# A decoder layer's mixture-of-experts output: rows accumulated in the output tensor instead of an internal copy of it

## The reference

```python
x = x + einsum('bse,ed->bsd', mix, w_out)            # "x2": one row for each token
h = rmsnorm(x, ln2_w)
logits = h @ w_router + b_router                      # 32 experts
top_vals, top_idx = top_k(logits, 4); gates = softmax(top_vals)
# for each expert e, over the tokens that chose it:
gu = h @ w_gate_up[e] + b_gate_up[e]
g = minimum(gu[:, :1024], 7); u = clip(gu[:, 1024:], -7, 7)
y = ((u + 1) * g * sigmoid(1.702 * g)) @ w_down[e] + b_down[e]
x[token] += gate * y                                  # four such rows are added to each token
```

## Time and profile before

| | us |
|---|---|
| median of three runs | 2045.23 (2040.22 to 2046.78) |
| the profiled execution | 2041.34 |
| its span, from first to last instruction | 2039.6 |
| TensorE matmul busy | 1899.4 (93%) |
| VectorE busy | 1277.3 (63%) |
| ScalarE busy | 1050.6 (52%) |
| GpSimd busy | 402.3 (20%) |
| DMA, mean | 246 GB/s, 501.81 MB |

### The profile page before, as it was taken

The page is one execution under the profiler, slowest core; times in us unless marked ns, Lnnn a source line. Parts: engine busy times, 40 slices in busy tenths (PEclk is TensorE's granted clock), DMA queues, the critical chain, the costliest instruction groups (busy, mean ns, idle before and its releaser), DMA issues.

```text
span 2039.6 us, 51127 instructions
## 1 busy us (share of the span) xinstructions
PE 1899.4 (93%) x20629; PEld 1761.9 (86%) x20629; DVE 1277.3 (63%) x2642; ACT 1050.6 (52%) x1442; POOL 402.3 (20%) x302
## 2 busy tenths in 40 slices
PE   6999988979968999999999999999999999989982
PEld 4777756658858999999999999999999999988982
DVE  4543647764378555566665567776677687776681
ACT  5574335552105444455555556555665665655661
POOL 4010000001002111111111112213243243333241
PEclk9999999989968999999999999999999999999996
DMA  4111010015377788889999899999999999999994
GB/s 141 52 42 42 21 62 1 2 46 189 137 260 246 262 280 280 272 274 304 306 306 306 303 310 312 312 327 336 371 354 372 371 353 371 370 351 369 369 346 114
DMA packets 251771, 501.81 MB, mean 246 GB/s; under 512 B 13025, under 2 KB 33809, under 8 KB 251585
## 3 DMA queue, kind: packets, MB, share of 16 engines
q1 hardware_dynamic: 231376, 446.73, 60.4%
q0 software_dynamic: 20256, 51.73, 11.7%
q10 hardware_dynamic: 48, 2.10, 0.3%
HBM read 471.16 MB, written 52.43 MB: 257 GB/s over the span
## 4 chain that ended last, share of the span: by engine, by line
PE 54%; DVE 4%; DMA 4%; issue 4%; SPq 2%; ACT 1%; POOL 0%; DVEq 0%; ACTq 0%; POOLq 0%
PE E_p_d L1945 22%; PE E_p_g L1934 5%; PE E_p_g L1937 5%; PE E_p_g L1936 5%; PE E_p_u L1937 5%; PE E_p_u L1934 5%; PE E_p_u L1936 5%; DMA E_w_st<-in_w_down 4%; DVE E_w_lo L1775 3%; SPq L1570 2%; PE E_p_t L1916 2%; PE E_p_t L1901 2%; ACT E_w_hi L1689 1%; DVE E_up L1835 0%; DVE E_gate L1823 0%
## 5 line engine op out<-in xcount | busy, mean ns | idle before, releaser
L1775 DVE SCALAR_TENSOR_TENSOR E_w_lo<-E_w_st,E_w_hi 128x2048 f16<-128x2048 f32 x260 | 594.8, 2288 | 60.3 <-ACT E_w_hi L1689 56.6
L1689 ACT ACTIVATE E_w_hi<-E_w_st 128x2048 f16<-128x2048 f32 x260 | 493.0, 1906 | 142.4 <-PE E_p_g L1937 95.7
L1945 PE MATMUL E_p_d<-E_a_f,E_w_st 128*128 128x160 f32 (+6 forms) x4096 | 536.3, 291 | 21.7 <-DMA E_w_st<-in_w_down 13.4
L1945 PEld LDWEIGHTS E_p_d<-E_a_f,E_w_st 128*128 128x128 f32 x4096 | 521.2, 193 | 29.2 <-DMA E_w_st<-in_w_down 16.2
L1934 PE MATMUL E_p_g<-E_x_hi,E_w_hi 128*128 128x160 f16 (+6 forms) x2048 | 373.0, 224 | 7.2 <-DVE E_w_lo L1775 7.2
L1934 PE MATMUL E_p_u<-E_x_hi,E_w_hi 128*128 128x160 f16 (+6 forms) x2048 | 371.7, 223 | 5.0 <-DVE E_w_lo L1775 5.0
L1936 PE MATMUL E_p_g<-E_x_lo,E_w_hi 128*128 128x160 f16 (+6 forms) x2048 | 373.0, 224 | 0.0
L1937 PE MATMUL E_p_g<-E_x_hi,E_w_lo 128*128 128x160 f16 (+6 forms) x2048 | 372.9, 224 | 0.0
L1937 PE MATMUL E_p_u<-E_x_hi,E_w_lo 128*128 128x160 f16 (+6 forms) x2048 | 371.6, 223 | 0.0
L1936 PE MATMUL E_p_u<-E_x_lo,E_w_hi 128*128 128x160 f16 (+6 forms) x2048 | 371.6, 223 | 0.0
L1633 POOL DMA_INDIRECT sum_rows<-E_y_rows,E_idx_out x66 | 169.0, 2561 | 596.6 <-ACT E_y_rows L1707 586.4
(11 more groups left out here) (375 smaller groups left out, 2758.7 us busy)
## 6 DMA issues: line engine op xcount, KB each, us to landing
E_w_st<-in_w_gate_up SPq DMA_DIRECT2D x130, 2048.0 KB, 15.7
E_w_st<-in_w_down SPq DMA_DIRECT2D x64, 2048.0 KB
A_w_st<-in_w_in SPq DMA_DIRECT2D x20, 512.0 KB, 3.9
sum_rows<-C_x SPq DMA_DIRECT2D x10, 512.0 KB, 5.8
A_x_rows<-in_x SPq DMA_DIRECT2D x8, 512.0 KB, 8.2
C_x_res<-in_x SPq DMA_DIRECT2D x8, 512.0 KB, 4.7
x_rows<-C_x SPq DMA_DIRECT2D x8, 512.0 KB, 5.0
h_rows<-C_h SPq DMA_DIRECT2D x8, 512.0 KB, 4.6
```

The lines of the kernel that those rows point to most:

```text
L1689: act.activation(w_hi[c % RI][:], staged(c % NG), ACT.Copy, scale=SW).then_inc(hi_s, 1)
L1775: dve.scalar_tensor_tensor(out=w_lo[c % RI][:], in0=staged(c % NG), scalar=SW, in1=w_hi[c % RI][:], op0=ALU.mult, op1=ALU.subtract, accum_ ...
L1945: ins = pe.matmul(banks[:, h, 0:w], staged(c)[:, k, h * P:(h + 1) * P], x[:, k, 0:w], start=h == 0 and k == 0, stop=k == KT - 1, skip_grou ...
```

## The change

The output projection's rows are written to the output tensor itself, and the experts' scatters accumulate there. `sum_rows` with its spare rows is gone. The scatter's bounds check gets the limit 1023 and leaves out lanes beyond it instead of calling them an error, so the padding lanes, which still point to rows 1024 and up, are written nowhere. Stage F is gone. The number of transfers, their waits and their order in stage E stay.

```diff
                     sp.dma_start(m.x2_d[q * P:(q + 1) * P, :], x2[q % 2][:]).then_inc(x2_out[q % 2], 16)
-                    sp.dma_start(m.sum_d[q * P:(q + 1) * P, :], x2[q % 2][:]).then_inc(sum_out[q % 2], 16)
-                    if q < NB:
-                        sp.dma_start(m.sum_d[S + q * P:S + (q + 1) * P, :], x2[q % 2][:]).then_inc(sum_out[q % 2], 16)
+                    sp.dma_start(a.out[0, q * P:(q + 1) * P, :], x2[q % 2][:]).then_inc(sum_out[q % 2], 16)
...
-                sp.wait_ge(sum_out[i], 16 * (T // 2 + 1))
+                sp.wait_ge(sum_out[i], 16 * (T // 2))
...
-                    dve.wait_ge(sum_out[t % 2], 16 * (t // 2 + 1))
+                    dve.wait_ge(sum_out[t % 2], 16 * (t // 2))
...
-            token_max, row_max = pool.to_reg(S - 1), pool.to_reg(S + CHUNK - 1)
+            token_max = pool.to_reg(S - 1)
...
-                    pool.indirect_dma_start(m.sum_d, bass.IndirectOffsetOnAxis(ap=idx_out[:, b:b + 1], axis=0),
-                                            y_rows[:, b, :], None, bounds_check=row_max, oob_is_err=True,
+                    pool.indirect_dma_start(a.out[0], bass.IndirectOffsetOnAxis(ap=idx_out[:, b:b + 1], axis=0),
+                                            y_rows[:, b, :], None, bounds_check=token_max, oob_is_err=False,
                                             compute_op=ALU.add).then_inc(scattered, 16)
...
-                    pool.dma_start(m.sum_d[0:S, :], m.x2_d).then_inc(restored, 16)
+                    pool.dma_start(a.out[0], m.x2_d).then_inc(restored, 16)
...
-def stage_f(nc, m, a):
...
-            sp.dma_start(a.out[0, 0:S // 2, :], m.sum_d[0:S // 2, :]).then_inc(done[0], 16)
...
-            act.dma_start(a.out[0, S // 2:S, :], m.sum_d[S // 2:S, :]).then_inc(done[1], 16)
...
-    m.sum_d = nc.dram_tensor("sum_rows", (S + CHUNK, D), F32).ap()
...
-    if "F" in stages:
-        stage_f(nc, m, a)
```

More of the change, by code:

```diff
@@ L1997, in _ @@
             if_any(pe, n_items, run)
-def stage_f(nc, m, a):
[L2002 to L2007, removed]
-            sp.dma_start(a.out[0, 0:S // 2, :], m.sum_d[0:S // 2, :]).then_inc(done[0], 16)
-            sp.wait_ge(done[0], 16)
-        @block.scalar
-        def _(act):
-            act.dma_start(a.out[0, S // 2:S, :], m.sum_d[S // 2:S, :]).then_inc(done[1], 16)
-            act.wait_ge(done[1], 16)
 class Memory:
```

## The result

The changed kernel takes 2013.48 us (median; 2010.76 to 2016.19) where the kernel before, beside it, takes 2044.31 (four runs, the three of before given above among them). The ratio is 0.9852 with an interval of 0.9836 to 0.9868: faster by 1.5%. The profiled execution took 2016.19 us, the longest of its four.

What follows compares the result with a forecast made beforehand. DMA traffic, padding scatters included, made weight loads late for TensorE in narrow items, and a copy followed the last barrier. 9.5 + 15.8 + 3.0 = 28.3 us off 2041.34 gave 2013.0, taken as 2013.5; range 2009 to 2021.

Steps and rivals of the forecast that it cites:

- The loads' lateness: Narrow items of stage E: weight loads no longer late for the down projection, 9.5 us gained (8.4 to 9.9).
- The DMA need: Stage E, items of width 112 and 96: DMA time per item falls from 38.6 to between 34.7 and 36.8 us.
- The last copy: Stage F at the end: the copy goes and the preceding barrier becomes the end, 15.8 us gained (15.0 to 15.9).
- The last scatter: End of stage E: with fewer real lanes the final scatter lands sooner, 3.0 us gained (0 to 3.9).
- Rival (a): End of stage E: GpSimd's drain hides the last landing, so its 3.0 us are not gained; 2016.0 us, chance 0.20.
- Stage C: Two padding writes go and eight change target; hidden by TensorE's out projection, 0 gained (at most 1.7 us without it).
- The sum: Whole kernel: 9.5 + 15.8 + 3.0 = 28.3 us off the profiled 2041.34, time 2013.0.
- The median above the profile: Whole kernel: median stood 3.9 us above the profiled execution; if from narrow-item lateness, it goes; 2013.5 taken.
- The clock in the slices: TensorE's granted clock, second half of the span: read as full speed but for two slices near the end.
- (b): Stage E's narrow items: loads stay late, only the end is gained; 2022.5 us, or 2026.4 by the median; chance 0.10.
- (d): Stage E's scatters: the check drops no lanes, which still cost full packets; copy alone gained, 2025.5 us; chance 0.03.
- (c): Stage E's scatters: accumulating into the output costs more per row, making it slower; decides from 61 ns a row; chance 0.03.

Runs made afterwards that it cites:

- the skipping alone: Kernel before with only the scatter's bounds check set to 1023 and leaving out lanes beyond; internal target and last copy stay: 2026.46 us against 2040.46, ratio 0.9924.
- The two half runs: Kernel before, still writing 64 padding lanes per narrow item, on the second column's partitions 0 to 63 (2038.52 us) or 64 to 127 (2028.06 us).
- the last experiment: Changed kernel without the eight small VectorE reductions per item that look for the largest float16 weight (first four chunks keep them): 2005.56 us, ratio 0.9804 to the kernel before.
- the copy alone: Kernel before without its last copy; output gets x after the output projection, experts' sums stay internal, all 256 lanes scattered: 2026.32 us, ratio 0.9919.
- the late wait: Changed kernel with GpSimd's last wait for the scatters moved behind stage E's closing barrier: 2009.51 us against 2045.19 of the kernel before, ratio 0.9834.
- the run on the internal tensor: Skipping and copy removal together on the kernel before, scatters still going to the internal tensor: 2013.76 us, ratio 0.9860, beside 2012.11 of the changed kernel.

## Why the prediction was right, point by point

The time, 2013.5 predicted and 2013.48 measured, agrees better than the sum behind it deserves. The steps one by one:

*The loads' lateness.* 9.5 us predicted (8.4 to 9.9), 10.16 found in the profile, 10.18 with the skipping alone. The working by item lengths held: every narrow item fell to the length that the trace of before showed for its undisturbed ones, also those whose delay I had read out of pairs. The 0.3 us more lie mostly in the item at the change of width, which by GpSimd's copies takes 36.14 us and not 36.52; the 0.4 us kept back for a thin margin were not needed. The clock's dip went with the wait, as read: from 1640 to 1970 us it is granted in full in all seven profiles without waits for the loads, and dips in the three with them. One reading was wrong: the slow down projection at 1911 does not stand behind the longest wait. That one, 4.1 us, ends at 1872.6, and its down projection took 12.7 us at 0.87 of full speed; the one at 1911 took 14.3 us behind a wait of 2.7 us, and the one at 1834, also behind 2.7 us, the full clock's 11.1. So the waits bring the dips, but how deep one is does not follow from the wait just before it.

*The DMA need.* Right in its result, wrong in its reasoning. I set it by the number of lanes, a middle between bytes and packet times, and left the uneven engines out of the sum. The two half runs show that the fullest engines decide: 96 lanes fewer were worth 1.8 of the 10.2 us on one side and all of them on the other. The change comes out well because real lanes fill an item from the front and the second column is empty, so that the fullest engines have half of what they had: first to last packet of the last scatter took 3.4 us where it took 6.2. Counted by lanes, 92 of 256, it would be 2.3. For the need of an item the last experiment gives an estimate of about 36 us. It lies in both ranges of the prediction, 34.7 to 36.8 by lanes and 35.5 to 37.1 by the fullest engines, so it does not choose between them; that 35.8 was near enough is in part luck. The sum of how far the loads fall back was also wrong: 5 x 1.2 + 5 x 2.1 + 6 x 0.3 are 18.3 us and not 14. No term of the forecast used it.

*The last copy.* 15.8 predicted, 15.5 with the copy alone. Nothing took its place.

*The last scatter.* 3.0 predicted, 2.7 measured (skipping alone; the two end pieces together 18.15). Rival (a), that the drain hides it, did not happen: the drain took 3.09 us in both kernels and began 2.6 us sooner behind the issue. With the late wait it began earlier still, was recorded as 6.8 us long, and ended 2.1 us sooner.

*Stage C.* Zero predicted. From its first load to the first cut there are 218.6 us before, 219.6 and 215.9 in the changed kernel's two profiles, 215.9 to 220.6 over all ten: no gain or loss can be told within that.

*The sum.* 28.3 predicted for the three terms; the traces show 10.16 + 18.15 = 28.3. The profiled execution moved by 25.2 only, because 3.2 us were lost ahead of the experts, and the medians by 30.8.

*The median above the profile.* This step was wrong. I took the runs' spread for lateness in the narrow items, which would go with it. It stayed: 6.6 us before, 5.4 after. The last ten items sum to 367.66 to 367.76 us in every profile without waits for loads (but the one with fewer reductions), while the part ahead of the experts varies by 7 us. The 0.5 us that I added was a guess between two cases, and that the median met it is luck.

*The clock in the slices.* The earlier trace rows was misread: there are no two slices near the end below nine tenths, only the last one (6), behind the last items. The dips of the narrow items are in the earlier trace rows, and the argument rests on these.

*Rivals.* (b), loads late for another reason, and (d), lanes not dropped, fall with the skipping alone and q0's 33.94 MB; (c), a dearer target, with the run on the internal tensor. The wide items were to stay and did, 938.72 and 938.64 us for 21 distances; the narrow ones move 358 to 360 GB/s, a little over the 355 that I had named as a sign.

## What to carry to other kernels

Padding that is carried by a transfer cost nothing here where TensorE set the pace, and 10 us where the loads did: compare what an item wants of the DMA engines with what its compute takes, item by item, and add up only the lengths above the pace of an undisturbed one. Before counting lanes saved, ask on which partitions they lie: the fullest engines set the time. A copy behind the last barrier is worth its whole length, since nothing lies beside it. A last wait ahead of that barrier is worth less than it lasts: moving 4.4 us of it gave 2.0.

## What the runs showed of the hardware

A skipped lane of a scatter costs next to nothing on the DMA engines, as for the gathers of the earlier trace rows: the last scatter of the changed kernel has 92 rows and 164 skipped lanes, and its row packets took 2.53 of the 2.66 us that all its 288 packets took of the 16 engines. Skipping does not shorten GpSimd's issue, 1.6 us each at the end with 256 real rows or with 92. The time of a scatter goes by the partitions of its lanes: GpSimd went on 7.5 us behind the second issue with 156 lanes of which 128 lie on the low partitions, 6.94 with 256 lanes on all, and 6.35 with 156 of which 92 lie on the high ones. GpSimd's drain behind the block with indirect transfers took 3.09 us in all nine profiles in which their landing had been waited for, and 6.82 in the one in which it had not, three of them beside its own issuing. And the part ahead of the experts, the same code on the same inputs but for stage C's writes, took between 665.2 and 672.2 us, first item included.
